# The low halves of the squared activations, pairs 2 to 31: formed by GpSimd in place of VectorE

## What is computed

```python
def squared_relu_mlp(h, w1, w2):
    return jnp.square(jax.nn.relu(h @ w1)) @ w2
...
        h = modulate(rms_norm(x, norm2_gain[layer]), sh2, sc2)
        x = x + g2[:, None, :] * squared_relu_mlp(h, w_ff1[layer], w_ff2[layer])
```

## Time and profile before

| | us |
|---|---|
| Median of 3 runs | 2527.88 |
| Lowest, highest | 2524.41, 2530.48 |
| The profiled execution | 2518.72 |
| Its span | 2516.9 |
| Busy in the span: PE, DVE, ACT, POOL | 2411.5, 1891.1, 1005.4, 368.3 |
| Granted TensorE clock, mean | 0.99 of full speed |

### The profile page before, as it was taken

The page is one execution under the profiler, slowest core; times in us unless marked ns, Lnnn a source line. Parts: engine busy times, 40 slices in busy tenths (PEclk is TensorE's granted clock), DMA queues, the critical chain, the costliest instruction groups (busy, mean ns, idle before and its releaser), DMA issues.

```text
span 2516.9 us, 36905 instructions
## 1 busy us (share of the span) xinstructions
PE 2411.5 (96%) x14008; PEld 2094.7 (83%) x14008; DVE 1891.1 (75%) x2143; ACT 1005.4 (40%) x1243; POOL 368.3 (15%) x154
## 2 busy tenths in 40 slices
PE   5999999999999999999899999999998999999997
PEld 3689888888888887787799999999987888888885
DVE  4356557777777535667889898989878889889988
ACT  4244322222322223225555555555553333343433
POOL 0100243333333443343100000000000000000000
PEclk9999999999999999999999999999999999999998
DMA  9945543333333652465365656565669888998883
GB/s 363 365 126 166 189 162 118 105 104 108 101 108 117 209 192 92 160 209 189 129 243 197 247 190 249 185 247 189 233 248 326 301 318 288 369 340 282 320 304 128
DMA packets 186344, 536.06 MB, mean 213 GB/s; under 512 B 15600, under 2 KB 15856, under 8 KB 179056
## 3 DMA queue, kind: packets, MB, share of 16 engines
q1 hardware_dynamic: 185792, 533.89, 60.0%
q10 hardware_dynamic: 432, 0.54, 0.1%
HBM read 467.26 MB, written 67.12 MB: 212 GB/s over the span
## 4 chain that ended last, share of the span: by engine, by line
PE 39%; issue 27%; DVE 13%; POOL 9%; DMA 8%; ACT 2%; SPq 1%; POOLq 0%; DVEq 0%; ACTq 0%
POOL w_lo L549 9%; PE banks L2192 6%; PE banks L2193 6%; PE banks L2194 6%; DVE w_lo L1460 5%; DMA raw<-in_w_stream 4%; PE banks L2156 2%; PE banks L2158 2%; PE banks L2157 2%; DMA ada_w<-in_w_ada 2%; PE banks L1773 2%; PE banks L1775 2%; PE banks L1774 2%; DVE raw L1467 1%; DVE half L1421 1%
## 5 line engine op out<-in xcount | busy, mean ns | idle before, releaser
L868 ACT ACTIVATE w_hi<-raw 128x1024 fp32r<-128x1024 f32 x434 | 451.9, 1057 | 423.1 <-PE banks L2194 226.7
L1460 DVE TENSOR_TENSOR w_lo<-raw,w_hi 128x1024 fp32r<-128x1024 f32 x434 | 523.6, 1219 | 82.6 <-ACT w_hi L868 82.6
L583 ACT ACTIVATE w_hi<-raw 128x1024 fp32r<-128x1024 f32 x186 | 197.4, 1061 | 736.4 <-PE banks L1761 487.7
L549 POOL TENSOR_TENSOR w_lo<-raw,w_hi 128x1024 fp32r<-128x1024 f32 x144 | 353.3, 2454 | 819.8 <-ACT w_hi L583 819.8
L2192 PE MATMUL banks<-w_hi,hid 128*128 128x512 f32 x896 | 351.5, 392 | 13.1 <-DVE w_lo L1460 6.2
L2193 PE MATMUL banks<-w_lo,hid 128*128 128x512 f32 x896 | 350.3, 391 | 0.0
L2194 PE MATMUL banks<-w_hi,hid 128*128 128x512 f32 x896 | 350.3, 391 | 0.0
L1759 PE MATMUL banks<-h_hi,w_hi 128*128 128x512 f32 x720 | 289.1, 402 | 0.0
L2156 PE MATMUL banks<-h_hi,w_hi 128*128 128x256 f32 x960 | 274.5, 286 | 12.4 <-DVE w_lo L1460 6.8
L1761 PE MATMUL banks<-h_hi,w_lo 128*128 128x512 f32 x720 | 281.0, 390 | 0.0
L1760 PE MATMUL banks<-h_lo,w_hi 128*128 128x512 f32 x720 | 280.6, 390 | 0.0
(11 more groups left out here) (277 smaller groups left out, 4470.8 us busy)
## 6 DMA issues: line engine op xcount, KB each, us to landing
raw<-in_w_stream SPq DMA_DIRECT2D x440, 512.0 KB, 4.8
hid<-hid_kept SPq DMA_DIRECT2D x112, 1024.0 KB, 7.1
ada_w<-in_w_ada SPq DMA_DIRECT2D x160, 512.0 KB, 5.0
hid_kept<-half SPq DMA_DIRECT2D x32, 1792.0 KB, 6.8
ada_w<-in_w_ada SPq DMA_DIRECT2D x64, 256.0 KB, 6.5
x_tok<-in_x SPq DMA_DIRECT2D x4, 1024.0 KB, 9.1
x_res<-in_x SPq DMA_DIRECT2D x4, 1024.0 KB, 8.0
x_kept<-x_res SPq DMA_DIRECT2D x4, 1024.0 KB, 9.7
```

Of the source, the lines that this page charges most:

```text
L549: pool.tensor_tensor(w_lo[:, r % 2], raw[:, r], w_hi[:, r % 2].bitcast(F32), ALU.subtract).then_inc(lo_done, 1)
L868: act.activation(operand_w(par, i)[0], raw_of(o), ACT.Copy).then_inc(hi_done, 1)
L1460: dve.tensor_tensor(lo, raw_of(OPERAND[i // 2] + i % 2), hi.bitcast(F32), ALU.subtract).then_inc(lo2_done, 1)
```

## The change

`half_low(m)` for m = 2 to 31 goes from VectorE to GpSimd. GpSimd executes them in a loop behind its last weight subtraction, each as soon as `half_hi` has reached m + 1; the data, the result and the semaphores are the same. `half_low(0)` and `half_low(1)` stay on VectorE.

```diff
@@ -563,6 +563,9 @@
             for r in (2, 3):
                 lo_unit(U_MLP // 4 + 1, r)
+            for m in range(2, PAIRS):
+                pool.wait_ge(half_hi, m + 1)
+                pool.tensor_tensor(half_r[:, 1:8, 1], half[:, 1:8, 1], half[:, 1:8, 0], ALU.subtract).then_inc(half_ready, 1)
...
@@ -1515,7 +1518,8 @@
                 operand_low(g, par, 4)
-                half_low(2 * g if g else 1)
+                if g == 0:
+                    half_low(1)
                 sum_t4(g, 0)
...
@@ -1533,8 +1537,6 @@
                 operand_low(g, par, 10)
-                if g:
-                    half_low(2 * g + 1)
                 operand_low(g, par, 11)
...
@@ -1556,8 +1558,6 @@
                 operand_low(g, par, 4)
-                if after_f1:
-                    half_low(2 * g)
                 sum_t4(g, 0)
...
```

## The result

The changed kernel takes 2550.75 us in the median of its runs (2548.52 to 2555.69), the kernel before 2528.2 us beside it: a ratio of 1.0093, 95% interval 1.0074 to 1.0113, or 22.6 us more. The profiled execution of the changed kernel took 2550.95 us, 0.2 us from its median. That of the kernel before was 9.2 us under its median, so the two traces differ by more (32 us) than the timed runs do.

The account below looks back on a forecast made before the run. PE, busy 96%, was taken as the bound, so changes pay only where it stands still. 14 groups x 3.5 = 49 us, plus about 2 for the last pair, gave 51 over the median 2527.9: 2579 us, range 2552 to 2600.

Parts of the forecast that it names:

- The hold: While GpSimd subtracts 1792 elements, VectorE is shut out for 3.8 us, where the removed instruction cost it 1.93 us.
- The first half: Pair 2g, behind unit 4's low half: VectorE, PE at unit 5 or 6, and the store all 1.9 us late.
- The second half: Pair 2g+1: unit 10's low half 3.5 us late, PE stops about 1.8 us, VectorE 1.6 us later from unit 11.
- Does the idle time give it back?: At the group's end: no, VectorE begins the next group about 3.5 us late, waiting for a later-issued weight load.
- the loop over units 12 and 13: Weight load issued behind these units, 1.9 + 1.6 = 3.5 us late, lengthens each group's period by 3.5 us.
- the 2 us of the last pair of halves: In the second product's first group, the last pair's swapped subtractions add about 2 us.
- VectorE catches up: Rival: at most group boundaries the store's chain counts; with the first half alone, 28 us more, 2556; chance 0.20.

Follow-up runs that it names:

- e1_first: Changed kernel, but GpSimd subtracts only each group's first half (pairs 2, 4, ... 30), the second being back on VectorE: 2551.61 us, ratio 1.0100.
- e4_after5: Kernel before, all subtractions on VectorE, with each group's first half moved behind unit 5's low half, so its store leaves later: 2564.26 us, ratio 1.0144.
- e5_pad5: Kernel before, with about 2.0 us of repeated subtraction on VectorE ahead of unit 5's low half in groups 1 to 14: 2549.54 us, ratio 1.0090.
- e8_pad11: Kernel before, with about 3.6 us of repeated unit 11 subtractions on VectorE behind the second half's low half, groups 1 to 14: 2526.02 us, ratio 0.9995.
- e2_second: Changed kernel, but GpSimd subtracts only each group's second half (pairs 3, 5, ... 31), the first being back on VectorE: 2525.64 us, ratio 0.9993.
- e3_memset: Changed kernel, with GpSimd writing zeros into the low halves of pairs 2 to 31 in place of subtracting: 2508.41 us, ratio 0.9929.

## Why the prediction was wrong, point by point

- **The hold** was right: 3.8 us taken for 1792 elements, 3.89 and 3.55 us measured in the group, 3.0 to 3.9 over all 30. GpSimd was let in between two VectorE instructions and shut VectorE out, as the rows of before had it. VectorE's busy time rose by 51 us, forecast 55.
- **The first half** was right, 1.9 us a group: 1.94 us in the traces, and e1_first gives the whole cost. Its reason was half of the truth. It took VectorE's delay as the cause and the store's as a companion; e4_after5 and e5_pad5 show that each alone costs as much.
- **The second half** was right as far as unit 10: GpSimd's hold there, VectorE 1.6 us late from unit 11 on, and a stop of PE, 1.29 us instead of 1.8.
- **The step that failed** is the one headed "Does the idle time give it back?": "that load was already the last to arrive", so being issued 3.5 us later it would arrive 3.5 us later. The load's time from issue to use isn't fixed: 8.25 us before, 7.8 in the changed kernel (1545.20 less its issue at 1537.44), 5.7 in e8_pad11. It lands some 5 us behind the store in front of it. So the loop over units 12 and 13 doesn't exist at this length, VectorE's lateness after unit 10 is taken up (3.7 us of it in e8_pad11), and the term of the second half is 0 and not 1.6 us a group: 14 x 1.6 = 22 us too much. PE's stop at unit 10 is given back as well: in e2_second it takes the place of PE's waits at units 5 and 6 and for `mod`.
- Of the remaining 6 us between 51 - 22 = 29 and the measured 22.6, about 4 are the first half's term: 1.9 us a group was forecast, and against the periods of e2_second and e8_pad11 the changed kernel's is 1.6 to 1.7 us longer, 22 to 23 us in all. That leaves next to nothing for the 2 us of the last pair of halves, which no run here measured by itself.
- **The rival** "VectorE catches up" gave 2556, 28 us, by just this count, with a chance of 0.20. It spoke of the store's chain at most boundaries, which is what the runs show. Its evidence was in the rows: the load was waited for only 8 times, one of them 4.7 us long and the other 7 together 5.5 us, while ScalarE's wait stood at 3.4. And weight loads of the same 512 KB took between 3.6 and 8.8 us from issue to landing in the one group of the rows, so a fixed time was not to be read from one of them.
- The range ended at 2552, 4 us under that rival's own time, and missed by 1.3 us.

## What to carry to other kernels

An engine's idle time is worth what stands behind it: here a delay ahead of a point where two chains meet with no slack cost in full, and one ahead of an engine's long wait cost nothing as long as no transfer in the chain left later. Before a transfer is put into a loop at its whole time, see whether its time from issue to landing is the same in all rows; if it varies, it waits for something else, and issuing it later may be free. And on a busy VectorE, a subtraction of two SBUF tensors moved to GpSimd wasn't relief but twice the time: 1.93 us on VectorE became about 3.7 us of standing still.

## What the runs showed of the hardware that was not expected

A GpSimd instruction that writes 1792 elements a partition and reads nothing took 1.60 us and left VectorE's 1.22 us instructions beside it unchanged, while the subtraction of the same size took 4.08 us at least and held VectorE until its own end, for 3.0 to 3.9 us. A weight load of 512 KB took between 5.7 and 8.25 us from issue to use, and what was nearly constant was its landing 3.8 to 5.8 us behind that of a 1.8 MB store. And a store that left earlier did not always land earlier: in e3_memset the second store left 2.5 us sooner behind its split than before (3.38 against 5.87) and landed 13.03 us behind it, before 12.79.
